# A depthwise convolution on TensorE: from two-phase split products to four-phase plain fp32

## The reference, cut to what matters

```python
h = x @ w_pw1 + b_pw1
a, g = jnp.split(h, 2, axis=-1)
h = a * jax.nn.sigmoid(g)
h = causal_depthwise_conv(h, w_dw) + b_dw      # 31 taps, each channel by itself
h = jax.nn.silu(layer_norm(h, ln_g, ln_b))
return h @ w_pw2
```

## Time and profile before

| | |
|---|---|
| median of three runs | 2538.86 us |
| the profiled execution, its own time | 2539.48 us |
| span of its trace, first to last instruction | 2537.7 us |
| PE matmul busy | 2515.6 us, 99% |
| PE weight loads busy | 2312.0 us, 91% |
| DVE busy | 1955.7 us, 77% |
| ACT busy | 1201.1 us, 47% |
| conv taps on PE, layer 0 | from 100.24 us to 164.87 us |
| conv taps on PE, layer 3 | from 1997.93 us to 2062.77 us |

### The profile page before, as it was taken

How to read it: one execution, slowest core, us unless ns; L and a number is a source line. 1 busy time by engine, 2 the same in 40 slices (tenths; PEclk the granted TensorE clock), 3 DMA queues, 4 the chain that set the end, 5 groups by cost and what they waited for, 6 DMA issues and landing times. The chain is left out here.

```text
span 2537.7 us, 41266 instructions
## 1 busy us (share of the span) xinstructions
PE 2515.6 (99%) x17241; PEld 2312.0 (91%) x17241; DVE 1955.7 (77%) x2571; ACT 1201.1 (47%) x1960; POOL 1.4 (0%) x10
## 2 busy tenths in 40 slices
PE   9999999999999999999999999999999999999999
PEld 7899999889888899998898899998898999999888
DVE  6989999578454679995784479996677979999576
ACT  6766444436233254443362254444356766444335
POOL 0000000000000000000000000000000000000000
PEclk9999999999999999999999999999999999999999
DMA  5203333324232233333233224333222203333322
GB/s 157 74 11 100 108 108 101 108 83 133 92 99 84 84 92 101 108 105 104 83 100 100 92 66 125 101 108 108 92 92 93 67 26 100 101 109 101 108 82 77
DMA packets 267054, 240.10 MB, mean 95 GB/s; under 512 B 14908, under 2 KB 212852, under 8 KB 266740
## 3 DMA queue, kind: packets, MB, share of 16 engines
q1 hardware_dynamic: 266292, 236.94, 30.1%
q10 hardware_dynamic: 576, 0.52, 0.1%
HBM read 233.21 MB, written 2.10 MB: 93 GB/s over the span
## 5 line engine op out<-in xcount | busy, mean ns | idle before, releaser
L1786 DVE TENSOR_TENSOR w_lo<-raw,w_hi 128x1024 fp32r<-128x1024 f32 x287 | 345.2, 1221 | 265.1 <-ACT w_hi L1309 264.6
L1309 ACT CAST w_hi<-raw 128x1024 fp32r<-128x1024 f32 x287 | 294.9, 1046 | 375.2 <-DMA raw<-in_ffn_w_down_dram 106.4
L879 PE MATMUL psum<-h_hi,w_lo 128*128 128x512 f32 x872 | 341.4, 392 | 0.0
L881 PE MATMUL psum<-h_hi,w_hi 128*128 128x512 f32 x872 | 339.3, 389 | 0.0
L880 PE MATMUL psum<-h_lo,w_hi 128*128 128x512 f32 x856 | 333.2, 389 | 0.0
L1024 PE MATMUL psum<-a_hi,w_lo 128*128 128x256 f32 x1088 | 280.0, 285 | 5.2 <-DVE w_lo L1786 3.6
L1024 PE MATMUL psum<-a_hi,w_hi 128*128 128x256 f32 x1088 | 276.6, 283 | 0.0
L1190 PE MATMUL psum<-h_hi,w_hi 128*128 128x256 f32 x768 | 217.3, 283 | 0.0
L1191 PE MATMUL psum<-h_hi,w_hi 128*128 128x256 f32 x768 | 217.3, 283 | 0.0
L1024 PEld LDWEIGHTS psum<-a_hi,w_lo 128*128 128x128 f32 x1088 | 208.6, 192 | 7.4 <-issue 3.7
L1321 ACT CAST w_hi<-w_hi_f 128x1024 fp32r<-128x1024 f32 x96 | 101.0, 1052 | 230.1 <-DVE w_hi_f L1814 230.1
(11 more groups left out here) (362 smaller groups left out, 6490.4 us busy)
## 6 DMA issues: line engine op xcount, KB each, us to landing
raw<-in_ffn_w_gate_dram SPq DMA_DIRECT2D x176, 256.0 KB, 3.0
raw<-in_ffn_w_up_dram SPq DMA_DIRECT2D x176, 256.0 KB, 3.4
raw<-in_ffn_w_down_dram SPq DMA_DIRECT2D x176, 256.0 KB, 3.2
raw<-in_a_w_pw_dram SPq DMA_DIRECT2D x94, 256.0 KB, 3.1
raw<-in_ple_w_gate_dram SPq DMA_DIRECT2D x64, 256.0 KB, 3.3
raw<-in_b_w_in_dram SPq DMA_DIRECT2D x64, 256.0 KB, 3.0
raw<-in_c_w_in_dram SPq DMA_DIRECT2D x48, 256.0 KB, 2.9
raw<-in_b_w_out_dram SPq DMA_DIRECT2D x32, 256.0 KB, 3.1
```

Source lines behind the costliest of these rows:

```text
L879: pe.matmul(bank(grp.g, j), st_lo, mv_hi, start=(k == 0), stop=False, skip_group_check=by_tiles(grp))
L881: done = pe.matmul(bank(grp.g, j), st_hi, mv_hi, start=False, stop=(ku == last and a == UK - 1), skip_group_check=by_tiles(grp))
L1309: act.copy(hi_u[u % RING], raw_u[u % RING]).then_inc(hi_ready, 1)
L1786: dve.tensor_tensor(lo_u[u % RING], raw_u[u % RING], hi_u[u % RING].bitcast(F32), ALU.subtract)\
```

## The change

The PE share of the convolution is written anew, and with it what feeds and drains it. DVE keeps tiles 0 and 1. Tiles 2 to 7 go to PE whole, all 31 taps, as plain fp32 (no high and low parts, so no `conv_hi`, `conv_lo`, split taps or diagonals). Tiles 2 to 6 use four row groups of 32 rows x 128 columns (`quad_tap`): 34 steps, each with one fp32 matmul for each of the four groups, 128 columns moving, each group into a PSUM bank of its own. Tile 7 uses two groups of 64 rows in two segments of 256 tokens (`pair_tap`): 32 steps, two matmuls each. DVE makes all blocks of a tile with one instruction (`make_blocks`). PSUM is emptied by small copies of 32 x 128 (or 64 x 128) straight to their place, 16 for a tile and 4 for a half, shared between ACT (`moved_high`, partly `moved_low`) and DVE; the DMAs that turned the phases are gone. A segment takes the banks of the last but one, and waits for its 16 copies. The centre moves into tile 5 (segment 3, after step 14), `conv_stats` of half 0 into the last segment after step 12. Blocks of tiles 2 to 6 lie in `a`; `a_hi` and `a_lo` begin 64 bytes further on, and `h` and all behind it stay where they are.

```diff
-TAPS_PE = 27
-PHASED = ((4, 0), (5, 0), (3, K_SHARED), (6, 0))
-TILE_ROWS = P // 2
+PHASES = 4
+ROWS = P // PHASES
+STEPS = TAPS_A + PHASES - 1
+QUADS = (2, 3, 4, 5, 6, 7)
+PAIR_ROWS = P // 2
+PAIR_STEPS = TAPS_A + 1
+SEGMENTS = ((0, None), (1, None), (2, None), (3, None), (4, None), (5, 0), (5, 1))
+CENTRE_IN, CENTRE_AT = 3, 14
+STATS_AT = 12
+A_SHIFT = 16
...
+        sb("a_pad", A_SHIFT)
         a_hi, a_at = sb("a_hi", DT * SEQ, F32R)
         a_lo, _ = sb("a_lo", DT * SEQ, F32R)
-        sb("a_end", TILE_ROWS)
+        rep, _ = sb("rep", ROWS)
+        sb("h_pad", ROWS - A_SHIFT)
...
+        def moves(s, i, high):
+            n, h = SEGMENTS[i]
+            n_q, size, at = n_phases(n), P // n_phases(n), SEGMENT * (h or 0)
+            y = by_phase(tiles(h_f32, CONV_Y + QUADS[n]), n_q)
+            return [(y[r * size:(r + 1) * size, n_q - 1 - j, at:at + SEGMENT],
+                     segment_bank(s, i, r)[j * size:(j + 1) * size])
+                    for r in range(n_q // 2 * high, n_q // 2 * (high + 1)) for j in range(n_q)]
...
-                        if s.kind == "mixer_out" and s.layer % 3 == 0 and grp.index == 1 and ku == AHEAD:
-                            for n in range(len(PHASED)):
-                                turn_phases(s, n)
...
-            def phase_tap(s, n, e):
...
-                for w, x in ((0, 1), (1, 0), (0, 0)):
-                    for r in range(2):
-                        moving = conv_split(n, x)[r * TILE_ROWS:(r + 1) * TILE_ROWS, at:at + HALF]
...
+            def quad_tap(s, i, e):
+                n = SEGMENTS[i][0]
+                for r in range(PHASES):
+                    moving = rows(conv_phases(n), r)[:, e % PHASES, e // PHASES:e // PHASES + SEGMENT]
+                    block = rows(tap_blocks(n), r)[:, e * ROWS:e * ROWS + P]
+                    last = pe.matmul(segment_bank(s, i, r), block, moving, start=(e == 0), stop=(e == STEPS - 1))
                 return last
...
             def conv_taps(s):
...
+                for i, (n, h) in enumerate(SEGMENTS):
+                    if i < 2:
+                        take_half(s.taps_g + i)
                     else:
+                        pe.wait_ge(moved_high, moved(s, i - 2))
+                        pe.wait_ge(moved_low, moved(s, i - 2))
+                    if i == CENTRE_IN + 1:
+                        pe.wait_ge(centre_saved, c + 1)
+                    pe.wait_ge(conv_phased, len(QUADS) * c + n + 1)
+                    pe.wait_ge(blocks_made, len(QUADS) * c + n + 1)
+                    for e in range(STEPS if h is None else PAIR_STEPS):
+                        last = quad_tap(s, i, e) if h is None else pair_tap(s, i, e)
+                        if i == CENTRE_IN and e == CENTRE_AT:
                             centre(s)
+                        if i == LAST and e == STATS_AT:
+                            conv_stats(s, 0)
                     last.then_inc(taps_done, 1)
...
+                        conv_by_phase(s, 4)
+                        conv_by_phase(s, 5)
                         split_more(AHEAD)
...
+                        for i in range(2):
+                            move(s, i, 1)
+                            move(s, i, 0)
+                        move(s, 2, 0)
                         save_centre(s)
+                        conv_squares(s)
...
+            def make_blocks(s, n):
...
+                own.add(dve.memset(blocks[:, 0:edge], 0.0))
+                own.add(dve.memset(blocks[:, TAPS_A + edge:TAPS_A + 2 * edge], 0.0))
+                dve.tensor_tensor(blocks[:, edge:edge + TAPS_A], many(pattern, TAPS_A),
+                                  taps.broadcast_to([P, TAPS_A, width]), ALU.mult).then_inc(blocks_made, 1)
...
             def conv_norm(s):
...
+                move_half(s, 5)
+                add_half(s, 5)
+                add_half_square(s, 5)
                 half_root(s, 0)
                 half_scale(s, 0, 0)
                 half_scale(s, 0, 1)
+                move_half(s, 6)
+                add_half(s, 6)
                 half_lo_pair(s, 0, 0)
```

More of the change, by code:

```diff
@@ L381, in tap_block @@
[L381 to L401, removed]
+        BLOCK_WORDS = BLOCKS * ROWS
@@ L403, in prm_taps, with moved, mean_bank, square @@
+        def moved(s, i):
+            return len(SEGMENTS) * (s.layer // 3) + i + 1
+        def mean_bank(s):
+            return bank(s.taps_g, 0, 2).rearrange("p (h s) -> p h s", h=2)[:, :, SEQ // PHASES:SEQ // PHASES + HALF]
+        def square(m):
+            return tiles(h_f32, m - TILES)
         def prm_taps(s):
@@ L916, in centre @@
             def centre(s):
+                pe.wait_ge(moved_low, moved(s, CENTRE_IN - 1))
                 pe.wait_ge(ysum_ready, s.layer // 3 + 1)
-                pe.matmul(bank(s.taps_g + 1, 0), ones_r[:, :], ysum[:, :], start=True, stop=True).then_inc(centre_done, 1)
+                for h in range(2):
+                    last = pe.matmul(mean_bank(s)[:, h], ones_r[:, :], hcol(ysum, h), start=True, stop=True)
+                last.then_inc(centre_done, 1)
             def conv_stats(s, h):
+                pe.wait_ge(moved_high, moved(s, LAST - 1 + h))
                 pe.wait_ge(conv_sums, 4 * (s.layer // 3) + 2 * h + 1)
@@ L950, in conv_taps, with pair_tap @@
+            def pair_tap(s, i, e):
+                n, at = SEGMENTS[i][0], e // 2 + SEGMENT * SEGMENTS[i][1]
+                for r in range(2):
+                    own = slice(r * PAIR_ROWS, (r + 1) * PAIR_ROWS)
+                    last = pe.matmul(segment_bank(s, i, r), tap_blocks(n)[own, e * PAIR_ROWS:e * PAIR_ROWS + P],
+                                     conv_phases(n)[own, e % 2, at:at + SEGMENT], start=(e == 0), stop=(e == PAIR_STEPS - 1))
+                return last
             def conv_taps(s):
-                c, n_diags, n_diag = s.layer // 3, 2 * (len(PHASED) - 1) + len(LAST_PARTS), 0
+                c = s.layer // 3
@@ L1422, in save_centre, with move @@
+            def move(s, i, high):
+                act.wait_ge(taps_done, moved(s, i))
+                for y, out_of in moves(s, i, high):
+                    last = act.copy(y, out_of)
+                last.then_inc(moved_high if high else moved_low, 1)
             def save_centre(s):
                 act.wait_ge(centre_done, s.layer // 3 + 1)
-                act.activation(mean[:, :], bank(s.taps_g + 1, 0), ACT.Copy, scale=2.0).then_inc(centre_saved, 1)
+                act.activation(mean[:, :].rearrange("p (h s) -> p h s", h=2), mean_bank(s), ACT.Copy, scale=2.0)\
+                    .then_inc(centre_saved, 1)
@@ new lines, in move, with centre_sum @@
+            def move(s, i, high):
+                dve.wait_ge(taps_done, moved(s, i))
+                for y, out_of in moves(s, i, high):
+                    last = dve.tensor_copy(y, out_of)
+                last.then_inc(moved_high if high else moved_low, 1)
+            def centre_sum(s):
+                own.settle()
+                wait_moved(s, 0)
+                wait_moved(s, 1)
+                for m in range(2):
+                    own.add(dve.scalar_tensor_tensor(tiles(tmp, 4 + m), conv_tile(2 + m), conv_bias(s, 2 + m), conv_tile(m),
+                                                     ALU.add, ALU.add))
@@ L2253, in convolve @@
                         lo_to(min(lo_end[0] + 1, lo_end_at))
[L2254 removed]
+                    for m in (m0, m0 + 1):
                         x = conv_x[:, m, PAD - taps + 1 + k:PAD - taps + 1 + k + SEQ]
```

468 lines of the change are left out of this document (159 added, 309 removed).

## The result

The changed kernel takes **2518.58 us** (median of four runs, 2517.4 to 2519.47) against 2538.74 (2538.58 to 2539.81) beside it: a ratio of 0.9919, 95% interval 0.9902 to 0.9937, 20.2 us less. The forecast was 12.8 us less. The profiled execution took 2518.05 us, its span 2516.3.

The account below looks back on a forecast made before the run. PE, busy 99%, was taken as the bound. Conv work of 57.4 against 64.6 us gains 7.2, less 0.3 and 0.5 of waits: 6.4 a layer, 12.8 for two, giving 2526 us; range 2512 to 2580.

Parts of the forecast that it names:

- The forecast case: Tiles 2 to 6: four row groups run side by side, two passes a step; 66%, range 2512 to 2534 us.
- Quads: Taps of the five four-group tiles: 170 steps of two 0.119 us passes, 0.238 a step, 40.5 us a layer.
- Tile 7: Two segments of 32 steps with two groups, two passes a step: 128 x 0.119 = 15.2 us a layer.
- Centre, start, copies: Centre put at 0.6 us, start and change of groups at 0.1 each, copies emptying PSUM at nothing.
- thin cover: At the centre, `ysum` and low copies come in time with 1 us to spare; 2 us late a layer gives 2530.
- Sums of half 0: Sums inside the last segment: 0.9 us of work, plus 0.3 us (0 to 1.5) of PE waiting for them.
- Behind the taps: Stops before the mixer: that for `a_hi` grows from 0.78 to 1.3 us, that of 1.00 stays; +0.5 together.
- Sums of half 1: Asked for later, after the taps; ready sooner than before, with no value given.
- second rival: Four-group steps: 16 instructions in 0.238 us may be too many; at 20 ns each 0.32 us, 2554 us; 18%.
- The shift: Moving `a_hi` and `a_lo` by 64 bytes is worth nothing; 6 us of possible gain kept at the lower end.
- Strict order: Rival: matmuls start in program order, groups overlap only in pairs, 0.46 to 0.49 us a step, 2607 us; 16%.
- Partial stacking: Rival: four row groups do not stack fully in the quad steps; 2534 to 2580 us, 18%.

Follow-up runs that it names:

- dve_moves: The changed kernel with the low copies of segment 4 moved from ScalarE to VectorE; 2516.91 us (one run, on another chip than the changed kernel).
- after: The changed kernel as first measured; 2518.58 us, ratio 0.9919 to the kernel before.
- after_again: The changed kernel once more, unchanged, on one chip with the kernel before; 2520.45 us, ratio 0.9923.
- no_shift: The changed kernel with `a` back at its old place (A_SHIFT = 0) and `h` where it was; 2523.54 us, ratio 0.9933.
- shift_all: The changed kernel with 64 bytes of padding ahead of every buffer and none in front of `a`; 2522.95 us (one run, another chip).
- fewer_groups: The changed kernel with part of the taps left out: segments 0 to 4 work with 4, 3, 2, 1 and 2 row groups; 2541.61 us.
- by_product: The kernel before with all three fp32r products of one row group, then all three of the other, instead of alternating; 2540.11 us beside 2540.12.
- two_steps: The changed kernel with two steps of one row group in a row, then two of the next, in the four-group tiles; 2519.14 us.
- pool_lo: The changed kernel with `h` also moved by 64 bytes, plus the pair stages' `w_lo` subtraction of a unit's own three blocks on GpSimd; 2579.03 us.
- shift_h: The changed kernel with `h` moved by 64 bytes too, so `a` and `h` both lie 64 bytes off the weights; 2523.99 us, ratio 0.9936.

## Why the prediction was right, and where its terms were off

**The forecast case** came: four row groups side by side. The marks named for it are in the trace. Raw starts inside a segment are 112.081, .085, .091, .098 and then 112.193: four within 17 ns, not 10, and the next four after 0.112 us. Segments are 7.6 to 8.3 us apart (8.1 forecast), the taps end at 156.3 (158 forecast), the centre has no idle time ahead of it, and the stop in front of the mixer is 1.36 us (1.3 forecast).

**Quads, mis-sized.** 170 steps at 0.238 were to be 40.5 us; they took 38.8 in layer 0: 37.9 at 0.223 a step, and 0.9 of single pauses (below). I had two rows for a pass, 0.119 with row groups and fp32r and 0.111 for plain fp32 in the full array, and took the one with row groups. The number type and column count of the other was the right likeness, since groups turned out to cost nothing. Tile 7 likewise: 14.3 us, not 15.2. Together 2.6 us better in layer 0; in layer 3 pauses take 1.7 of them back. The 0.223 was my lower bound.

**Centre, start, copies.** The centre cost 0.60 us as put. The copies of 32 x 128 took 0.38 us each where I had 0.25 to 0.37, longer than the 0.367 of 128 x 256 that I took for a bound (the two of 64 x 128 took 0.27); ACT was through with segment 1 at 122.3 and `ysum` there at 124.6, so the thin cover held.

**Sums of half 0, mis-sized.** 0.9 us of work were 1.2, and the 0.3 us of waiting 0.9, within its bounds of 0 to 1.5. The cause is that two ends of a race moved by different amounts. With shorter steps segment 5 ends at 147.1, 2.4 us ahead of the 149.5 I had, and PE asks at 149.9. DVE, held by ACT's copies of segment 4, came only 0.9 us earlier than I had it (149.01 for 149.9) and had the first sum at 150.9. dve_moves shows that this is the whole of it.

**Behind the taps**: 1.36 and 0.87 us for 1.3 and 1.00.

**Sums of half 1, put at nothing.** Of the 2.5 us without work after the taps the two waits that I named make only 1.8. The other 0.7 is the wait for the sums of half 1 (L929, the row shown above). I wrote that these sums would be ready sooner and gave it no value; it was worth nearly 1 us a layer.

**Not priced: supply of instructions.** My second rival was that 16 instructions in 0.238 us are too many. The pace inside shows none of it, 14 ns an instruction. But there are single pauses, most of all in layer 3, where the profile names nothing that is waited for:

```profile
1986.65 4.50 PE L914 MATMUL psum<-a_f 32*128 32x128 f32 x147
1991.77 3.73 PE L914 MATMUL psum<-a_f 32*128 32x128 f32 x123 [0.61 <-issue]
```

In the eight conv layers of after, after_again, no_shift and shift_all such pauses sum to 0.1 to 2.1 us a layer, and differ between executions of one kernel. In fewer_groups, segment 1 with three groups has none, but neither has segment 1 of the changed kernel with four, so that settles nothing. Where they come from is not shown.

**The shift, a step that failed.** "So 64 bytes are worth nothing" rested on the taps of tile 7 with their offsets of 0 to 104 bytes. I took their spread for noise. It is none: every tap has the same duration in layer 0 and in layer 3, to 1 ns. That the addresses make it, as in the shift, is likely and not shown. Outside the two conv stretches the trace is 7.0 us shorter. Without the shift it is 2.4 shorter (shift_all: 0.7 between the layers, 1.7 behind them), most of which is the wait for the sums of half 1, and the other 4.6 are the shift. I had kept 6 us at the lower end. By the medians on one chip it is worth 3.1 us. Two executions of the same kernel differ by 1.9 us in the part behind layer 3 alone; 1.5 of that is the stretch at the lower clock.

The sum of 12.8 us became 14.5 in the layers (a better pass, a worse chain, and pauses) and 7.0 elsewhere, where the sum had nothing. The trace is 21.4 us shorter, 8.6 more than the sum. Of these only 1.7 lie in the stretches that the change is about; the rest is what the sum put at nothing. **Strict order** is refuted by by_product and two_steps, not only by the time. **Partial stacking**, 0.276 us or more a step, is refuted by 0.223 with two, three and four groups.

## What to carry to other kernels

Price a matmul in row groups by the plain row of the same type and column count: groups beside it were free here, in the three orders of issue tried, but with one or two of four the clock fell. Where two engines are nearly level, as TensorE and VectorE in the pair stages, a gain of one on paper can come back as pauses (a stage of 181.3 us became one of 180.5 to 181.1, not of 177), so look at the chain that feeds it before an effect of 1% is summed up over the whole kernel. Before two traces are compared to 1 us, look whether the clock fell in one of them. When a wait is removed, make the chain behind it earlier; asking later only moves it.

## What the runs showed of the hardware that I had not expected

- Row groups start out of program order: a group's matmul ran ahead of two that stand before it (by_product), and four records of one group in a row cost the others nothing (two_steps).
- A pass costs 0.112 us with 4, 3 or 2 groups of 32 rows, and with one at the full clock, so four groups give four times one. The Trainium skill, page "TensorE: Matmul & The Clock Gate", "Measured speedup vs the span model", has 3.07 for 512 columns; the runs here have 4 for 128 columns of plain fp32.
- The granted clock fell to 0.50 in fewer_groups after 7.6 us of two groups and 3.5 of one, while TensorE was never idle; in the segments with three and with four groups it stayed at 1.00.
- It also fell to 0.50 for 3.4 us right behind the taps of layer 3 in some executions and not in others of the same kernel (after_again and the changed kernel's first), which costs 1.5 us.
- 256 columns moving from an address 64 bytes off the weights' (mod 256) take 116.7 to 118.5 ns from start to start, not 120, and 512 columns 229 to 230, not 227.
- A subtraction of 128 x 1024 on VectorE took 1.84 us beside GpSimd's of 128 x 768 (pool_lo) and 1.22 without (shift_h).
